# VectorE's convolution taps moved into the set-up of the state space model, and all z units at the opening of the second block

## The reference

```python
u = rmsnorm_2(h, norm_mix_w[l])
proj = u @ w_in[l]
z, xbc, dt_raw, conf_in = jnp.split(proj, [D_SSD, D_SSD + D_XBC, D_SSD + D_XBC + SSD_HEADS], axis=-1)
y_ssd = ssd_mixer(z, xbc, dt_raw, ...)
y_conf = conformer_conv(conf_in, ...)
h = h + jnp.concatenate([y_ssd, y_conf], axis=-1) @ w_out[l]
h = h + peer_ffn(rmsnorm_2(h, norm_ffn_w[l]), ...)

def ssd_mixer(z, xbc, dt_raw, ...):          # state space model, 16 heads of 64
    xbc = silu(causal_depthwise_conv(xbc, conv_w, conv_b))          # 4 taps
    dt = softplus(dt_raw + dt_bias)
    y = ssd_chunked(x * dt, dt * a_neg, B, C) + d_skip * x          # chunks of 128 tokens
    y = y * silu(z)
    ...                                                             # norm by group

def conformer_conv(u, conv_w, conv_b, ln_g, ln_b):
    a, g = jnp.split(u, 2, axis=-1)
    h = causal_depthwise_conv(a * jax.nn.sigmoid(g), conv_w, conv_b)  # 31 taps
    ...                                                             # LayerNorm over 1024 features, then silu
```

## Time and profile before

| | |
|---|---|
| median of 3 runs | 1492.34 us (1490.55 to 1492.49) |
| profiled execution | 1492.37 us, span 1490.5 us |
| busy PE, PEld, DVE, ACT | 95%, 87%, 71%, 49% of the span |
| set-up and LayerNorm sum | 490.5 to 559.8 us of the span |

### The profile page before, as it was taken

One profiled execution on the slowest core, in us unless ns is written; L12 is line 12 of the kernel. 1 busy time (PEld: TensorE's weight loads), 2 busy tenths in 40 slices (PEclk: granted clock), 3 DMA queues, 4 the chain that ended last, 5 costly groups with the idle time before them and its releaser, 6 DMA issues.

```text
span 1490.5 us, 25207 instructions
## 1 busy us (share of the span) xinstructions
PE 1416.0 (95%) x10482; PEld 1291.8 (87%) x10482; DVE 1062.2 (71%) x1720; ACT 735.1 (49%) x1052; POOL 2.5 (0%) x8
## 2 busy tenths in 40 slices
PE   6999799998999968999999999999999999999997
PEld 5977699998999857799999999999987777888886
DVE  4565666546799676767899997788878898555554
ACT  4555556444667616556544445444444444444443
POOL 0000000000000000000000000000000000000000
PEclk8999899999999989999999999999999999999999
DMA  6332266664455002156465555555545555565653
GB/s 226 120 105 86 73 196 184 191 197 136 158 169 170 29 0 71 57 158 195 144 186 184 187 180 187 167 167 161 169 160 167 168 170 162 180 191 193 194 186 110
DMA packets 63617, 228.59 MB, mean 153 GB/s; under 512 B 7312, under 2 KB 8208, under 8 KB 63376
## 3 DMA queue, kind: packets, MB, share of 16 engines
q1 hardware_dynamic: 61776, 223.90, 47.5%
q10 hardware_dynamic: 1728, 3.09, 0.5%
HBM read 225.91 MB, written 1.05 MB: 152 GB/s over the span
## 4 chain that ended last, share of the span: by engine, by line
PE 89%; DVE 6%; ACT 3%; issue 1%; DMA 1%; ACTq 0%; DVEq 0%
PE ps L291 17%; PE ps L293 17%; PE ps L292 17%; PE ps L858 8%; PE ps L859 8%; PE ps L860 8%; PE ps L824 2%; PE ps L600 2%; DVE plain L1569 1%; DVE W L1347 1%; DVE RSI L1353 1%; PE ps L478 1%; PE ps L341 1%; DMA plain<-in_masks 1%; PE ps L299 1%
## 5 line engine op out<-in xcount | busy, mean ns | idle before, releaser
L1347 DVE TENSOR_TENSOR W<-raw,W 128x1024 fp32r<-128x1024 f32 x423 | 516.4, 1224 | 290.1 <-ACT W L904 288.8
L904 ACT ACTIVATE W<-raw 128x1024 fp32r<-128x1024 f32 x423 | 446.9, 1058 | 383.1 <-PE ps L860 208.0
L291 PE MATMUL ps<-XH,W 128*128 128x256 f32 (+1 forms) x1608 | 460.6, 286 | 7.9 <-DVE W L1347 5.2
L292 PE MATMUL ps<-XL,W 128*128 128x256 f32 (+1 forms) x1608 | 456.8, 284 | 0.0
L293 PE MATMUL ps<-XH,W 128*128 128x256 f32 (+1 forms) x1608 | 454.6, 283 | 0.0
L291 PEld LDWEIGHTS ps<-XH,W 128*128 128x128 f32 x1608 | 304.1, 189 | 10.2 <-issue 7.1
L293 PEld LDWEIGHTS ps<-XH,W 128*128 128x128 f32 x1608 | 306.3, 190 | 0.0
L292 PEld LDWEIGHTS ps<-XL,W 128*128 128x128 f32 x1608 | 304.8, 190 | 0.1
L858 PE MATMUL ps<-W,HH 128*128 128x512 f32 x512 | 205.6, 402 | 0.8 <-ACT hid L1312 0.8
L859 PE MATMUL ps<-W,HH 128*128 128x512 f32 x512 | 202.8, 396 | 0.0
L860 PE MATMUL ps<-W,HL 128*128 128x512 f32 x512 | 202.8, 396 | 0.0
(11 more groups left out here) (312 smaller groups left out, 1923.9 us busy)
## 6 DMA issues: line engine op xcount, KB each, us to landing
raw<-in_w_dn SPq DMA_DIRECT2D x128, 512.0 KB, 3.5
raw<-in_w_up SPq DMA_DIRECT2D x128, 512.0 KB, 3.5
raw<-in_w_ff SPq DMA_DIRECT2D x64, 512.0 KB, 4.2
raw<-in_w_in SPq DMA_DIRECT2D x57, 512.0 KB, 3.5
raw<-in_w_out SPq DMA_DIRECT2D x24, 512.0 KB, 3.4
raw<-in_w_q SPq DMA_DIRECT2D x16, 512.0 KB, 3.5
raw<-in_w_kv SPq DMA_DIRECT2D x4, 512.0 KB, 3.3
plain1a<-in_memT ACTq DMA_DIRECT2D x1, 1024.0 KB, 11.0
```

What stands on the lines that cost most here:

```text
L291: e.matmul(out, wh, xh, start=first, stop=False, skip_group_check=shared)
L292: e.matmul(out, wh, xl, start=False, stop=False, skip_group_check=shared)
L904: e.activation(W[:, u % NSLOT, 0, :], raw[:, u % NRAW, :], ACT.Copy).then_inc(s["hi"], 1)
L1347: e.tensor_tensor(W[:, u % NSLOT, 1, :], raw[:, u % NRAW, :], W[:, u % NSLOT, 0, :], ALU.subtract).then_inc(s["lo"], 1)
```

## The change

- The last 2 z units move to the opening, so that all 8 run there, the last two in bank 0; the order of weight units in memory changes with it. The splits of weights between the steps of `h_parts` and `h_high` move by a step or two. The GLU unit that uses bank 0 waits for the fourth SZ product.
- ScalarE's Silu of the 6 tiles of `SZ` in the set-up becomes two of 4 tiles; the Silu of the last 2 tiles, behind the LayerNorm's root, goes, and so do the weight splits there.
- VectorE's taps in the set-up: 8 become 18, 3 new ones stand ahead of L1614, 4 stay, 4 in each chunk become 8, 5 new ones follow each product with decays, and 12 stand ahead of the second chunk's state.
- The LayerNorm's sum takes tiles 6 and 7 ahead of 4 and 5.

```diff
-        za_bank = (2, 3, 1)
+        za_bank = (2, 3, 1, 0)
...
             first_pair(U_ZA, za_bank[0], 2, ZH, ZL)
-            for m in range(2, 6):
+            for m in range(2, 8):
...
-                if m == 5:
-                    e.wait_ge(s["zr"], 3)
+                if m == 4:
+                    e.wait_ge(s["zr"], 4)
...
-            for j in range(8):
+            for j in (0, 1, 2, 3, 6, 7, 4, 5):
                 e.wait_ge(cv[j], 31)
-                t = e.matmul(ps[2][:, 0:256], ones, CV[:, j, :], start=j == 0, stop=j == 7)
+                t = e.matmul(ps[2][:, 0:256], ones, CV[:, j, :], start=j == 0, stop=j == 5)
             t.then_inc(s["ln_mm"], 1)
-            next(z)
             e.wait_ge(s["xdt"], 6)
             column_sums(3, 256, SQ2, SQ_LN)
-            next(z)
...
             for c, _ in enumerate(h_high(1, T2, 272, U_F2)):
-                if c in (2, 5, 7):
-                    hi_to(U_ZA + 6 + (2, 5, 7).index(c))
+                if c in (1, 3, 5, 7):
+                    hi_to(U_ZA + 6 + c // 2)
...
-            e.wait_ge(s["zr"], 3)
-            e.activation(flat(SZ[:, 0:6, :]), flat(SZ[:, 0:6, :]), ACT.Silu).then_inc(s["z_out"], 1)
+            e.wait_ge(s["zr"], 4)
+            for i in (0, 4):
+                e.activation(flat(SZ[:, i:i + 4, :]), flat(SZ[:, i:i + 4, :]), ACT.Silu).then_inc(s["z_out"], 1)
...
-            hi_to(U_Z + 3)
             sqrt_table()
...
             root(N_LN, 3, 256, 1.0 / 1024, eps5)
-            hi_to(U_Z + 4)
-            e.wait_ge(s["unit"], U_Z + 2)
-            e.activation(flat(SZ[:, 6:8, :]), ps[6][:, :], ACT.Silu).then_inc(s["z_out"], 1)
...
             for c, _ in enumerate(h_parts(24, T2, "mixw", 272, 16)):
-                if c in (2, 5, 8):
-                    lo_to(U_ZA + 5 + c // 3)
-            for p in range(3):
+                if c in (2, 4, 6, 8):
+                    lo_to(U_ZA + 4 + c // 2)
+            for p in range(4):
                 e.wait_ge(s["unit"], U_ZA + 2 * p + 2)
...
-            some_taps(8)
+            some_taps(18)
             e.wait_ge(s["dt_a"], 3)
             e.scalar_tensor_tensor(DT, DT, 0.0, DA, ALU.max, ALU.add).then_inc(s["dt_v"], 1)
             e.wait_ge(s["dt_v"], 2)
             e.wait_ge(s["dt_a"], 4)
+            some_taps(3)
             e.scalar_tensor_tensor(t3(DX), t3(DT), -1.0, row3(AN[:, 0:16]), ALU.mult,
                                    ALU.mult).then_inc(s["dt_v"], 1)
...
                     if hf == 0:
-                        some_taps(4)
+                        some_taps(8)
                 if c < 2:
...
                                     spread(DC[0:n, c * 16:c * 16 + 16], n, 16), ALU.mult).then_inc(s["xde"], 1)
+                    some_taps(5)
+            some_taps(12)
             for hf in range(2):
                 dst = PREV[1][:, hf * 512:hf * 512 + 512]
...
-            lo_to(U_Z + 3)
             inverse(N_LN, 256)
-            lo_to(U_Z + 4)
```

More of the change, by code:

```diff
@@ L38 @@
 U_QK, U_FV, U_GU, U_MQ, U_KM, U_VM, U_WO, U_F1, U_F2 = 0, 6, 12, 15, 17, 19, 21, 29, 61
-U_ZA, U_GLU, U_XB, U_Z, U_OC, U_OS, U_WQ, U_SK, U_DN, U_UP, NU = 93, 99, 115, 131, 133, 141, 149, 165, 167, 295, 423
+U_ZA, U_GLU, U_XB, U_OC, U_OS, U_WQ, U_SK, U_DN, U_UP, NU = 93, 101, 117, 133, 141, 149, 165, 167, 295, 423
 NRAW, NSLOT = 4, 3
@@ L585, in tensor_program @@
                 h_unit(U_XB + m, ps[in2_bank(m)][:, 0:272], C272)
[L587 to L590, removed]
             def conv_taps():
@@ L608, in tap @@
                     next(taps, None)
-            z = z_units()
             e.wait_ge(s["xb"], 9)
@@ L1246, in scalar_program @@
                 square(SQ2[:, c:c + 2, 0:256], X[:, c:c + 2, :])
-            highs = h_high(2, T3, 256, U_Z + 2)
+            highs = h_high(2, T3, 256, U_XB + 16)
             for m in range(16):
@@ L2051 @@
         "w_out": a["w_out"][0].reshape(8, 128, 1024), "w_ff1": _units(a["w_ff1"][0]),
-        "w_ff2": _units(a["w_ff2"][0]), "w_in2": _units(np.concatenate([z[:, :768], conf, xbc, z[:, 768:]], axis=1)),
+        "w_ff2": _units(a["w_ff2"][0]), "w_in2": _units(np.concatenate([z, conf, xbc], axis=1)),
         "w_out2": np.concatenate([_units(w_out2[1024:]), _units(w_out2[:1024])]),
```

## The result

The changed kernel takes 1483.45 us in the median of 5 runs (1479.37 to 1484.54) against 1492.34 of the kernel before (5 runs, 1490.55 to 1493.16); the ratio is 0.9939, 95% interval 0.9923 to 0.9955. Forecast were 1483.4, in 1480.4 to 1488.0.

The account below looks back on a forecast made before the run. TensorE, busy 95% of the span, was taken to bound the kernel. From 1492.4, 7.5 lost in the opening less 18.0 gained before the scan gives -10.5; one clock fall adds 1.5: 1483.4 us, range 1480.4 to 1488.0.

Parts of the forecast that it names:

- The taps and the sum: End of set-up: VectorE's taps moved into its waits let the LayerNorm sum end earlier, centring 14.8 us sooner.
- The pitch of 0.40: VectorE's convolution taps in the set-up: one tap costs 0.40 us.
- Rival A: VectorE binds the set-up: six places overshoot by 0.3 to 0.5, 2 to 3 us in all, 1486; chance 0.09.
- The cover: Set-up: TensorE's own taps just hide VectorE's added taps, exact to hundredths of a us.
- The chain: LayerNorm steps from centring to scaling: column sums 2.0 us sooner and a weight split of 1.2 gone.
- The weight split: VectorE's split between reciprocal and scaling in the LayerNorm chain: its going gains 1.2 us.
- The wait before the first conformer unit: TensorE's wait behind the LayerNorm chain grows to some 4 us; clock cost taken as nothing, 1.5 at worst.
- The opening: Second block's start: two more z units cost 5.6 us, plus a new 1.9 wait before GLU, 7.5 together.
- rival B: Opening: splits of z units 5 to 7 are late as well, two waits, 4 to 5 us, 1488; chance 0.07.
- Rivals C and D: C: half clock lasts through the taps, 1496 and more, 0.03; D: scan and output give back 8 us, 1491, 0.03.
- Before the decay sums: Set-up: 3 taps (1.2 us) and the longer Silu (0.5) make TensorE wait 3.2 us, everything behind 1.7 later.
- The clock: A fall to half clock costs 1.5 us: likely (8 in 10) before the decay sums, even chances before GLU.

Follow-up runs that it names:

- Putting the split first: The changed kernel with VectorE's weight split for the first GLU unit ahead of the fourth SZ product: 1479.71 us, ratio 0.9911.
- second profile: The changed kernel run once more with no edit, for another profile: 1483.73 us, ratio 0.9938.
- taps alone: The kernel before with the change's tap counts and order of the LayerNorm sum, z units left as before: 1475.71 us, ratio 0.9894.
- the kernel with more taps: The changed kernel with 12 taps, not 8, behind each chunk's first product and the 12 ahead of the second chunk's state gone: 1483.69 us.
- the 3 taps behind: The changed kernel with the 3 taps ahead of dt times decay put behind it and the two products for the scan: 1480.99 us.
- z alone: The kernel before with all z units in the opening, taps and order of the sum unchanged: 1497.61 us, ratio 1.0044.

## Why the prediction was right

**The taps and the sum.** Forecast: centring 14.8 us earlier, which is 16.5 off the stage from sum to centring less 1.7 of delay before it. The stage is 16.50 shorter: 14.2 us of waits, and 2.3 because the sum before ran in pieces, the last eight matmuls in 3.78 us at half clock, where sixteen now take 3.62. From dt to the sum it takes 1.98 longer in one profile and 3.35 in the other (1.67 and 1.68): 14.5 and 13.2 net. The pitch of 0.40 held: 18 taps took 7.20 us. Rival A is out: the places shown were as tight as computed, and the kernel with 1.6 us too much in three of them lost nothing, since TensorE runs ahead of the products by a bank (3.0 us). The cover was better than my text said.

**The chain.** Forecast 3.2, measured 2.97 (10.55 to 7.58), less 0.26 on the way to the scan. The weight split by itself is not worth 1.2, as I had it: taken out alone it brought 0.6 in the profile and nothing in the medians, since ScalarE's own work behind the root takes its place. The move of z clears both engines. The wait before the first conformer unit is 4.2 us, as forecast, and the clock did fall behind it (0.50 from 563.0 to 569.9), which cost no more than the 0.26. I had put it at nothing.

**The opening.** Forecast 7.5 with a new wait of 1.9; measured 7.51, 7.52 and 1.91. Splits of z units 5 to 7 were on time, rival B is out. Putting the split first took 2.1 off.

Rivals C and D are out as well: no half clock lasted through the taps (all of 505.50 to 548.80 ran at 1.00 in the first profile, and the fall in the second cost 1.7), and what stands behind the chain gave nothing back but the 0.26.

**Before the decay sums the size was right and the wait was wrong.** I forecast a wait of 3.2 us and the stage 1.7 longer. It is 1.98 and 1.67 longer, but TensorE waited only 0.20 and 1.53. Its dt matmuls and first taps were slower themselves: in the first profile 7.6 and 8.9 us, before 5.6 and 7.6, at a granted clock of 0.50 from 494.8 to 505.0, before from 489.8 to 493.2. I had not seen the fall in the dt matmuls that the kernel before already has. VectorE's dt sum, which waits for them, was 2 us later with them, and so the 18 taps were no longer hidden by ScalarE: L1600 follows them without a wait (507.12), 1.7 behind the end of ScalarE's logarithm at 505.40. In the second profile the half clock lasts from 495.9 to 502.7, the dt sum is only 0.9 late, and VectorE and ScalarE run as forecast: the 3 taps stand 0.84 us behind L1600 until ScalarE's exponential is done (506.84), and L614 follows them, 16.43 us behind the first dt matmul (forecast 16.46). The halves of the change confirm the two terms apart: 0.50 with the longer Silu alone, 1.14 with the taps alone. So in the second profile the 1.7 is earned; in the first, 2.0 came another way, and that it lies near 1.7 is luck.

**The clock.** I counted one fall of 1.5 us and placed it behind the decay sums. Each of the two profiles has one extra, 1.7 us, the first behind the wait before GLU, the second behind the decay sums. That one such fall goes with each execution is argued, not shown: a third profile, that of the kernel with more taps, has the one at GLU too, but that with the 3 taps behind has neither. My chances were not multiplied out either: 8 in 10 and evens split the forecast's 0.78 into 0.31 for the set-up alone, 0.31 for both, 0.08 for none and 0.08 for GLU alone. The text has 0.36, 0.30 and 0.12 and no case for the last, which the first profile shows.

**The remainder.** In the touched stretch the change brought 8.1 and 8.2 us, forecast 9.0; the medians say 8.9. That the median met the forecast within 0.1 us is luck at this size: 0.8 of it lies in no stage that the forecast spoke of. Outside the stretch the profiles differ by up to 3 us with the same instructions in the same order, and behind the start of the scan it is the clock that differs. Two waits of TensorE are in every profile there, one of 2.6 to 2.7 us at 617 to 641 and one of 2.0 at 695 to 720. The nine profiles in which the clock falls behind both take 910.6 to 911.5 us from the scan's second call to the end; two in which it falls only behind the later one take 909.3 and 909.4; the first profile of the change, in which it falls behind neither, takes 907.6. Such a fall costs 1.4 to 1.7 us.

**What the forecast didn't ask** is whether both halves of the change earn their place. Its own terms said no: z costs 5.6 + 1.9 + 0.5 and returns 3.2. Taps alone at -17.0 and z alone at +4.9 us show it. The two sum to -12.0, and the change gives -8.9. Some 0.8 of the gap of 3.1 is that in taps alone z's unit already runs at full clock, so the chain's gain is not had twice (0.82 with the taps, 2.96 with z, 2.97 with both); 1.7 would be the extra fall of the clock, which neither half has in its profile; the rest, 0.6, is open.

## What to carry to other kernels

Work that is moved into an engine's waits for another costs nothing as long as each portion fits between two products, and more than fits is borne where the other engine has buffers ahead (here 3.0 us, of which 2.5 were tried); but a portion ahead of an instruction that the busiest engine waits for is on the path, however small (3 taps, 1.1 us). Filler that already sits in gaps of the critical chain should stay there until the gap is gone: moved to a dense stage it costs its full time (here 2.8 us a unit, where two units in the chain had cost 3.0 together), and it drags its bookkeeping into other queues, here a PSUM product that held back the next weight split. When a change has two halves, add up each alone, since a good sum can hide a bad half.

## What the hardware showed that I had not expected

The length of a wait alone did not decide whether the clock fell. The 2.6 us before z unit 4 was followed by a fall in all eleven profiles that have it; a wait of the same length at 617 to 641 in nine of twelve, and one of 2.0 at 695 to 720 in eleven of twelve. Before the decay sums 2.66 us in taps alone was not followed by one (40.00 us for the set-up behind it), nor was the 1.51 of the kernel before, but 1.53 us was in the second profile of the change. The 1.9 us before GLU was followed by a fall in two of five profiles. And the clock also fell without any wait ahead of it: during the 48 dt matmuls (128x16 each), 2.6 to 5.0 us after the first of them, in all twelve profiles. How long it then stayed at half, 3.4 to 10.2 us, differed between profiles and with it VectorE's dt sum came 5.8 to 7.9 us behind the first dt matmul.
